# FFN input projection by token in 512 columns, with the activations turned on TensorE, and FFN sublayers that begin with the first half of the tokens

## The reference

```python
def modulate(h, shift, scale):
    return h * (1 + scale[:, None, :]) + shift[:, None, :]

def swiglu_ffn(h, w_in, w_out):
    g, u = jnp.split(h @ w_in, 2, axis=-1)
    return (jax.nn.silu(g) * u) @ w_out

for i in range(DEPTH):
    mod = jax.nn.silu(c) @ w_ada[i] + b_ada[i]
    sh1, sc1, g1, sh2, sc2, g2, sh3, sc3, g3 = jnp.split(mod, 9, axis=-1)
    h = modulate(rms_norm(x, norm_pre[i, 0]), sh1, sc1)
    y = swiglu_ffn(h, w_ffn_in[i, 0], w_ffn_out[i, 0])
    x = x + 0.5 * g1[:, None, :] * rms_norm(y, norm_post[i, 0])
    ...   # the mixer likewise with sh2, sc2, g2; then an FFN with sh3, sc3, 0.5 * g3
```

## Time and profile before

| what | before |
|---|---|
| median of 3 runs | 1553.05 us (1551.29 to 1553.85) |
| profiled execution | 1553.27 us, of which the span that the trace shows is 1551.5 |
| TensorE (PE) busy | 1530.8 us, 99% |
| VectorE (DVE) busy | 1120.9 us, 72% |
| ScalarE (ACT) busy | 773.3 us, 50% |
| DMA moved | 343.69 MB, mean 222 GB/s |

### The profile page before, as it was taken

The page is one execution under the profiler, slowest core; times in us unless marked ns, Lnnn a source line. Parts: engine busy times, 40 slices in busy tenths (PEclk is TensorE's granted clock), DMA queues, the critical chain, the costliest instruction groups (busy, mean ns, idle before and its releaser), DMA issues.

```text
span 1551.5 us, 24340 instructions
## 1 busy us (share of the span) xinstructions
PE 1530.8 (99%) x10060; PEld 1389.1 (90%) x10060; DVE 1120.9 (72%) x1322; ACT 773.3 (50%) x959; POOL 165.6 (11%) x96
## 2 busy tenths in 40 slices
PE   7999999999999999999999999999999999999998
PEld 5999889998988889999899998899989888899986
DVE  5887766867897977677566776577878979664553
ACT  3544455556473456444454444554746544554433
POOL 0000002303311110000000000040324011000000
PEclk9999999999999999999999999999999999999999
DMA  9998956655677856788767887475567777456552
GB/s 341 308 311 277 324 160 217 177 150 182 214 246 227 269 165 218 254 265 274 239 194 249 278 264 251 125 216 161 170 195 237 234 247 242 152 180 187 179 188 95
DMA packets 196979, 343.69 MB, mean 222 GB/s; under 512 B 15731, under 2 KB 107123, under 8 KB 196869
## 3 DMA queue, kind: packets, MB, share of 16 engines
q1 hardware_dynamic: 178724, 276.07, 56.2%
q10 hardware_dynamic: 18144, 66.07, 13.1%
HBM read 341.05 MB, written 1.05 MB: 221 GB/s over the span
## 4 chain that ended last, share of the span: by engine, by line
PE 87%; DVE 8%; issue 2%; ACT 1%; DMA 1%; SPq 0%; POOL 0%; ACTq 0%; DVEq 0%; POOLq 0%
PE ps L692 10%; PE ps L695 10%; PE ps L694 10%; PE ps L709 6%; PE ps L708 6%; PE ps L707 6%; PE ps L1035 6%; PE ps L1036 6%; PE ps L1037 6%; PE ps L1098 4%; PE ps L1100 4%; PE ps L1099 4%; DVE w_lo L1458 2%; DVE ada_acc L1474 2%; PE ps L759 1%
## 5 line engine op out<-in xcount | busy, mean ns | idle before, releaser
L1458 DVE TENSOR_TENSOR w_lo<-w_raw,w_hi 128x1024 fp32r<-128x1024 f32 x480 | 614.0, 1297 | 157.5 <-ACT w_hi L1158 157.0
L1158 ACT ACTIVATE w_hi<-w_raw 128x1024 fp32r<-128x1024 f32 x490 | 506.8, 1052 | 356.5 <-DMA w_raw<-in_w_ffn_out 118.3
L692 PE MATMUL ps<-h_hi,w_hi 128*128 128x256 f32 x1408 | 398.5, 284 | 3.5 <-DVE w_lo L1458 2.8
L695 PE MATMUL ps<-h_hi,w_lo 128*128 128x256 f32 x1408 | 397.8, 283 | 0.0
L694 PE MATMUL ps<-h_lo,w_hi 128*128 128x256 f32 x1376 | 389.9, 283 | 0.0
L692 PEld LDWEIGHTS ps<-h_hi,w_hi 128*128 128x128 f32 x1408 | 270.7, 192 | 5.0 <-DVE w_lo L1458 4.0
L695 PEld LDWEIGHTS ps<-h_hi,w_lo 128*128 128x128 f32 x1408 | 270.8, 192 | 0.0
L694 PEld LDWEIGHTS ps<-h_lo,w_hi 128*128 128x128 f32 x1376 | 264.6, 192 | 0.2
L1098 PE MATMUL ps<-h_hi,w_hi 128*128 128x256 f32 x704 | 201.6, 286 | 0.0
L1099 PE MATMUL ps<-h_lo,w_hi 128*128 128x256 f32 x704 | 199.1, 283 | 0.0
L1100 PE MATMUL ps<-h_hi,w_lo 128*128 128x256 f32 x704 | 199.1, 283 | 0.0
(11 more groups left out here) (285 smaller groups left out, 1899.1 us busy)
## 6 DMA issues: line engine op xcount, KB each, us to landing
w_raw<-in_w_ffn_in SPq DMA_DIRECT2D x176, 512.0 KB, 4.7
w_raw<-in_w_in SPq DMA_DIRECT2D x168, 512.0 KB, 3.7
ada_slab<-in_w_ada ACTq DMA_DIRECT2D x126, 512.0 KB, 4.6
w_raw<-in_w_ffn_out SPq DMA_DIRECT2D x88, 512.0 KB, 3.9
ada_slab_first<-in_w_ada SPq DMA_DIRECT2D x16, 512.0 KB, 9.7
w_raw<-in_w_ssm_out SPq DMA_DIRECT2D x16, 512.0 KB, 4.3
w_raw<-in_w_out SPq DMA_DIRECT2D x16, 512.0 KB, 3.5
w_raw<-in_w_pool_out SPq DMA_DIRECT2D x8, 512.0 KB, 3.7
```

What stands on the lines that cost most here:

```text
L692: mm(out, wh[:, cs], HH[:, k, :], start=(k == 0 and t == 0), stop=False)
L695: ins = mm(out, wl[:, cs], HH[:, k, :], start=False, stop=(c != 0 and k == KD - 1 and t == 1))
L1158: fn(WH[:, n % N_HI, 0:width], RAW[:, n % N_RAW, 0:width], ACT.Copy).then_inc(w_hi, 1)
L1458: dve.tensor_tensor(WL[:, n % N_RAW, 0:width], RAW[:, n % N_RAW, 0:width], WH[:, n % N_HI, 0:width], ALU.subtract).then_inc(w_lo, 1)
```

## The change

Three parts, and one line.

1. **FFN input by token.** A chunk is now 256 rows of both the gate and the up columns (256 + 256), loaded by two DMAs of 256 KB. `token_chunk`, which the mixer had, does 12 matmuls of 512 columns per chunk with 128 tokens of h stationary and the weights moving. A unit's result lies by token in two banks (`unit_banks`). ScalarE's silu and VectorE's product (now `act_by_token`) come after the whole unit; then TensorE turns the product with four plain transposes (`act_turn`), and `act_hi` and `act_lo` are taken from PSUM. `act_turn` of a unit stands one chunk behind the unit's end, the last one in the output projection.
2. **Boundaries.** The shift row is summed once per boundary while the sublayer before still runs (`shift_sums`, four matmuls of 512 columns), and copied to SBUF (`shift_row`). VectorE makes normalised x plus shift by token (`h_full`, two instructions per half of the tokens, in place of the diagonal), and `h_turn` is eight plain transposes per half of the tokens; the one for the first tokens stands before the last three matmuls of the sublayer before.
3. **FFN begins with the first tokens.** `first_tokens` does for FFN and mixer what the mixer did: four chunks for tt = 0, gate_row_sums, `h_turn` for tt = 1, four chunks for tt = 1. ScalarE's and VectorE's order at an FFN's boundary becomes that of a mixer's.
4. The start of the work area is rounded up to 128 bytes, so that `act_hi` begins at 155,392.

```diff
-        work = (cursor[0] + 63) // 64 * 64
+        work = (cursor[0] + 127) // 128 * 128
...
-                        load(raw.rearrange("p (k n) -> p k n", k=4),
-                             w_ffn_in[l, f, rows, col:col + T].rearrange("(k p) n -> p k n", p=P))
+                        for k in range(2):
+                            rows = slice((2 * q + k) * P, (2 * q + k + 1) * P)
+                            v = w_ffn_in[l, f, rows, :].rearrange("p (g n) -> p g n", g=2)
+                            load(raw[:, k * HALF:(k + 1) * HALF].rearrange("p (g n) -> p g n", g=2),
+                                 v[:, :, u * T:(u + 1) * T])
...
+            def token_chunk(g, j, banks, hi, lo, kn, tts, lo_ready=None):
+                wh, wl = weights(g)
+                parts = [(kk, tt) for kk in range(2) for tt in tts]
...
+                for kk, tt in parts:
+                    k = 2 * j + kk
+                    out = PS[:, banks + tt, :]
+                    cs = slice(kk * HALF, (kk + 1) * HALF)
+                    mm(out, hi[:, k, tok(tt)], wh[:, cs], start=(k == 0), stop=False)
+                    mm(out, hi[:, k, tok(tt)], wl[:, cs], start=False, stop=False)
+                    if lo_ready is None:
+                        ins = lo_product(kk, tt)
+                if lo_ready is not None:
+                    lo_ready()
+                    for kk, tt in parts:
+                        ins = lo_product(kk, tt)
+                return ins
...
-                for kk, t in tiles:
-                    out, k, cs = halves(kk, t)
-                    mm(out, wh[:, cs], HH[:, k, :], start=(k == 0 and t == 0), stop=False)
-                    if c:
-                        mm(out, wh[:, cs], HL[:, k, :], start=False, stop=False)
-                    ins = mm(out, wl[:, cs], HH[:, k, :], start=False, stop=(c != 0 and k == KD - 1 and t == 1))
+                token_chunk(g, q, unit_banks(s, u), HH, HL, KD, (0, 1), ready).then_inc(w_used, 1)
+
+            def act_turn(s, u):
+                f = 2 * (s // 3) + (s % 3) // 2
+                pe.wait_ge(a32_ok.sem, a32_ok.at(f, u + 1))
+                if u >= 2:
+                    pe.wait_ge(al_ok.sem, al_ok.at(f, u - 1))
+                for j in range(2):
+                    for tt in range(TT):
+                        ins = pe.transpose(PS[:, turned_in(u), j * T + tt * P:j * T + (tt + 1) * P],
+                                           A32[:, u % 2, tt, j * P:(j + 1) * P], ident)
+                ins.then_inc(at_ps.sem, 1)
+
+            def first_tokens(s):
+                for tt in range(TT):
+                    if tt:
+                        gate_row_sums(s)
+                        h_turn(s, 1)
+                    pe.wait_ge(yg_ok.sem, yg_ok.at(s - 1, 3 + tt))
+                    for j in range(4):
+                        if j % 2 == 0:
+                            pe.wait_ge(hh_ok.sem, hh_ok.at(s, 2 * tt + j // 2 + 1))
...
+                        ins = token_chunk(BASE[s] + j, j, 6, HH, HL, KD, (tt,), ready if j % 2 == 0 else None)
+                        if tt:
+                            ins.then_inc(w_used, 1)
...
-            def shifts(b, tt):
...
-                for k in range(KD):
-                    mm(PS[:, 2 * tt + k // 4, (k % 4) * P:(k % 4 + 1) * P], part(0)[:, k * P:(k + 1) * P], ones,
-                             start=(k % 4 == 0), stop=False)
...
             def h_turn(b, tt):
-                pe.wait_ge(f_ok.sem, f_ok.at(b, tt + 1))
                 for half in range(2):
-                    for k in range(4 * half, 4 * half + 4):
-                        ins = mm(PS[:, 2 * tt + half, (k % 4) * P:(k % 4 + 1) * P], Y[:, tt, k * P:(k + 1) * P], DG[:, tt, :],
-                                 start=False, stop=(k % 4 == 3))
+                    pe.wait_ge(f_ok.sem, scaled(b, 2 * tt + half + 1))
+                    for k in range(4):
+                        ins = pe.transpose(PS[:, 2 * tt + half, k * P:(k + 1) * P],
+                                           Y[:, tt, half * HALF + k * P:half * HALF + (k + 1) * P], ident)
...
+            def shift_sums(t, bank):
+                column_sums(0, t, bank).then_inc(sh_ps.sem, 1)
...
                 if s:
-                    shifts(s, 0)
-                    h_turn(s, 0)
-                    shifts(s, 1)
-                    gate_row_sums(s)
-                    h_turn(s, 1)
-                for c in range(N_IN):
+                    first_tokens(s)
+                for c in range(4 if s else 0, N_IN):
+                    for u in ended_at(s, c, 2):
+                        act_turn(s, u)
...
+            def h_full(b, tt):
...
+                for half in range(2):
+                    cs = slice(half * HALF, (half + 1) * HALF)
+                    dve.scalar_tensor_tensor(Y[:, tt, cs], Y[:, tt, cs], RB[:, tt:tt + 1], SHROW[:, cs], ALU.mult, ALU.add)\
+                        .then_inc(f_ok.sem, 1)
```

More of the change, by code:

```diff
@@ L81, in unit_of, with ended_at, unit_banks, turned_in @@
     return FIRST_ORDER[c] if s == 0 else (c // 4, c % 4)
[L84 to L87 removed]
+def ended_at(s, c, later):
+    return [unit_of(s, c - later)[0]] if 0 <= c - later < N_IN and unit_of(s, c - later)[1] == 3 else []
+def unit_banks(s, u):
+    if u == 0 and s:
+        return 6
+    return 2 * u if u < EARLY and s == 0 else 2 * (u % 2)
+def turned_in(u):
+    return 2 if u == UNITS - 1 else 6 + u % 2
 COUNT = [N_MIX if s % 3 == 1 else N_FFN for s in range(SUBS)]
@@ L92, with is_dtff @@
 CHUNKS = BASE[SUBS]
+def is_dtff(g):
+    s = max(i for i in range(SUBS) if BASE[i] <= g)
+    return s % 3 == 1 and g - BASE[s] == at_unit("dtff")
 def landings(g):
     s = max(i for i in range(SUBS) if BASE[i] <= g)
-    return 2 if s % 3 == 1 and g - BASE[s] == at_unit("dtff") else 1
+    return 2 if is_dtff(g) or s % 3 != 1 and g - BASE[s] < N_IN else 1
 LANDED = [16 * sum(landings(h) for h in range(g % N_RAW, g + 1, N_RAW)) for g in range(CHUNKS)]
@@ L679, in ffn_in @@
-                if u >= (2 if s else EARLY) and q == 2:
                     pe.wait_ge(a32_ok.sem, a32_ok.at(f, u - 1))
-                wh, wl = weights(g)
-                bank = (2 * u if s == 0 and u < EARLY else 2 * (u % 2)) + q // 2
-                tiles = [(kk, t) for kk in range(4) for t in range(2)]
-                def halves(kk, t):
-                    k = 4 * (q % 2) + kk
-                    cs = slice(kk * T + t * P, kk * T + (t + 1) * P)
-                    return PS[:, bank, t * T:(t + 1) * T], k, cs
```

246 lines of the change are left out of this document (119 added, 127 removed).

## The result

The changed kernel takes 1564.03 us (median of 7 runs, 1558.71 to 1565.49), the kernel before 1553.51 (7 runs): slower, ratio 1.0062, 95% interval 1.0051 to 1.0074.

What follows compares the result with a forecast made beforehand. The prediction took TensorE's queue as the bound, busy 1530.8 of 1551.5 us. Its terms summed to -1.5 on 1553.3, giving 1551.8, or 1551.5 against the median, with an 8-in-10 range of 1541 to 1564.

Steps and rivals of the forecast that it cites:

- FFN input pitch: In the four FFNs' input, 2112 matmuls of 512 columns at .2267 replace 4224 of 256 at .1200: -26.5 us.
- alignment: Work area on a multiple of 128 bytes: 1728 matmuls with act or y stationary go from .2333 to .2267, -11.4 us.
- transposes: Turning the activations on TensorE: 11 units in each of 4 FFNs, .45 per batch of four transposes, +20 us.
- boundaries: Five sublayer boundaries: fourth chunk ends sooner despite a new idle time of 1.9 us at each, -10.1 us.
- gate_row's wait: Sublayers 2, 3 and 5: TensorE's transposes of unit 0 now wait for the row's DMA, +11 us, bounds 8 and 18.
- sublayer 0's wait: VectorE waits for slabs of w_ada, so TensorE meets the product of two units late: +1.9 us, bounds 0 and 3.
- clock: New idle times bring TensorE's granted clock to half behind three stalls and about half of the boundaries: +9 us, bounds 0 and 14.
- rival C: Act and y matmuls: the 64-byte offset isn't the cause of .2333, so alignment gives 0: 1563 us, chance .12.
- rival B: Sublayers 2, 3 and 5: gate_row waits longer for its load, 6 us each, clock at upper bound: 1563 us, chance .20.
- rival A: Whole kernel: idle times cost only themselves, clock 0, row's wait at its lower bound: 1540 to 1543 us, chance .27.
- Rival D: FFN input: matmuls of 512 columns cost .240, no cheaper per column, so its term is 0: 1578 us, chance .02.
- rival E: Boundaries: the second tokens' wait takes back all that the early start gives, +8 to +10, 1561 us, chance .05.

Runs made afterwards that it cites:

- e3: The kernel before with only the start of the work area rounded up to 128 bytes instead of 64: 1551.25 us, ratio .9989.
- g1 to g3: Work area's start 128 bytes further on, against the changed kernel: 1554.32 us; against the fastest version, only weight rings 128 bytes further on: 1551.24; everything: 1535.12.
- e1: The changed kernel with SP asking for the norm_post row one load earlier, ahead of chunk BASE+8's load: 1551.81 us, ratio .9995.

## Why the prediction was wrong

Forecast 1551.5, measured 1564.0, at the very edge of the range of 8 in 10 (1541 to 1564) and past it by .03; the side was wrong too, 1.5 below before where it came out 11 above. Step by step, against +11.5 of the profiled execution:

| term | forecast | measured | from |
|---|---|---|---|
| FFN input pitch | -26.5 | -26.3 | .1555 per chunk x 169 |
| alignment | -11.4 | -1 | pitch .2333 to .2327; e3 |
| transposes | +20 | +21 | .48 x 44 |
| shift sums | +4.6 | +4.6 | mixer stretches +.8, with the pitch |
| boundaries | -10.1 | -11.8 | -13.7 in all, less 1.9 counted under FFN input |
| gate_row's wait | +11 | +15 | 4.6, 4.6, 5.3 and .16 restarts |
| sublayer 0's wait | +1.9 | +2.6 | 2.33 and .25 |
| clock | +9 | +7.5 | 2.5 behind each of three waits |

**The step that failed is the alignment term.** It took the only visible difference between two groups of matmuls for the cause, at full size, and gave the other possibility .12 (rival C; its time, 1563, is where the result went). The observation was right (two pitches, .0066 apart), and that an address decides it too; but the modulus is 256 and relative to the moving operand, which both e3 and g1 to g3 show. The change moved the rest from 192 to 0 where 128 was wanted. With -1 in place of -11.4 the sum would have been 1562. The other seven terms missed by 2.7 together, as the +4 of gate_row's wait was partly cancelled by the boundaries and the clock; that these cancelled is luck. (The 1728 matmuls of this term are 1056 on act and 672 on y tiles, not 1248 and 480; the sum is right.)

**The wait moved onto TensorE** was found, with its place and its cause, and mis-sized by 4: I took 6.8 us from issue to start from sublayer 3 for two of them and let sublayer 5 keep its advantage. After the change SP issues at +24.0 rather than +23.3: the load ahead of the row is now two DMAs, which hold SP's queue for 1.24 where the one of before held it for .41. Sublayer 5 was as late as the others (5.3). So rival B's mechanism was at work, at 4.6 to 5.3 a wait and not at its 6. What I hadn't seen is that the silu waits almost as long for chunk 8: with the row alone repaired the time was 1552, not 1542. The prediction had it only in its last sentence, as a wait without a row of its own ("silu and product of a whole unit now lie in one chunk's time").

**The clock**: the size was nearly right, the distribution not. None of the five boundaries of this execution had clock .50, and each of the three long waits had it for twice as long as the earlier trace rows (6.8 against 3.4). Over 11 profiles with the five boundary waits in place (1.4 to 1.7 idle), clock .50 followed in 20 of 55 cases, at about 1.5 each. The same kernel differs in this from one execution to the next: e1's ten runs go from 1548.8 us at a mean granted clock of .999 to 1555.7 at .993. So rival A's premise (idle times cost only themselves) holds in some executions and not in others, and this is likely part of the 7 us between the fastest and the slowest run of the changed kernel (.994 and .991). The Trainium skill, "TensorE: Matmul & The Clock Gate", section "Part 4: PE-mode transpose", says that transposes don't count as busy for the clock as matmuls do. By it, the prediction had said, the term goes to its upper bound, +14, with the clock down behind all eight new idle times; the term came to +7.5. At the boundaries, where transposes stand beside the idle time, the clock was down in 20 of 55; that neither confirms the page nor refutes it, as no run here separates the transposes from the idle time.

**Pitch, transposes, boundaries** came out within 2 us each. The chain at the boundary, made by hand from the mixer's rows, was off by .15 at its end. Rival D (.240 for 512 columns) is refuted by the pitch of .2271, and rival E by the boundaries, which gained 13.7.

## What to carry to other kernels

When TensorE is made to need another engine's result sooner, follow that result's queue back on every engine: a wait for a DMA that cost nothing before (here 4.39 for a row) becomes TensorE's own. Here moving two instructions in two queues turned +10 us into -10. And where a pass over weights is split in two by tokens, its buffers come free only in the second pass, so ask when the loads behind them are issued. When two groups of equal matmuls run at different pitch, try the address of one against that of the other before building a term on it. And a wait of some 1.6 us on TensorE can cost nearly twice its length by the clock, in some executions and not in others (20 of 55 here), so compare medians.
